# Ten moves in the order of work of a three-layer transformer kernel: rotations, first loads, a bias table, norms and idle products

## The reference

```
x = layer_norm(x)
for l in (0, 1):
    x = layer_norm(alpha * x + hybrid_mixer(x))            # ln 0
    x = layer_norm(alpha * x + memory_attention(x, mem))   # ln 1
    x = layer_norm(alpha * x + conv_ffn(x))                # ln 2
h = rms_norm(x)
q, kv, kr, dil, mq, gates = split(h @ w_in)                # third layer
x = x + rms_norm(merge(gates, mla(q, kv, kr), dilated(dil), mem_attn(mq, mem_2)) @ w_o)
x = x + rms_norm(conv_ffn(rms_norm(x)))
```

## Time and profile before

| what | value |
|---|---|
| runs shown | 1657.93, 1658.93, 1662.61 us; median 1658.93 |
| the profiled execution | 1660.57 us, span 1658.7 us |
| TensorE busy | 1629.4 us, 98% |
| VectorE, ScalarE, GpSimd busy | 1157.1, 868.7, 40.0 us |
| chain that ended last | TensorE 88%, VectorE 9%, issue 2%, ScalarE 1% |
| weights | 525 loads of 512 KB, 4.3 us to landing at the median |
| memory traffic | 305.84 MB, mean 184 GB/s |

### The profile page before, as it was taken

One profiled execution on the slowest core, in us unless ns is written; L12 is line 12 of the kernel. 1 busy time (PEld: TensorE's weight loads), 2 busy tenths in 40 slices (PEclk: granted clock), 3 DMA queues, 4 the chain that ended last, 5 costly groups with the idle time before them and its releaser, 6 DMA issues.

```text
span 1658.7 us, 32250 instructions
## 1 busy us (share of the span) xinstructions
PE 1629.4 (98%) x13674; PEld 1591.4 (96%) x13674; DVE 1157.1 (70%) x1734; ACT 868.7 (52%) x1302; POOL 40.0 (2%) x59
## 2 busy tenths in 40 slices
PE   9999999999999999999999999999999999999998
PEld 8999999999999999999999999998989999999998
DVE  6678778657566767877874966677576545877777
ACT  5456544645444454555355654445745555465554
POOL 3000000003000000000000000000000000000000
PEclk9999999999999999999999999999999999999999
DMA  9854457536656465545664465555545454546562
GB/s 314 288 178 153 153 196 249 187 126 193 227 175 207 161 236 163 162 144 190 203 239 144 160 222 181 201 181 164 178 146 167 152 178 140 179 153 204 178 205 100
DMA packets 82798, 305.84 MB, mean 184 GB/s; under 512 B 10688, under 2 KB 10816, under 8 KB 80480
## 3 DMA queue, kind: packets, MB, share of 16 engines
q1 hardware_dynamic: 77008, 279.44, 50.7%
q0 software_dynamic: 5648, 24.35, 4.9%
HBM read 300.52 MB, written 6.29 MB: 185 GB/s over the span
## 4 chain that ended last, share of the span: by engine, by line
PE 88%; DVE 9%; issue 2%; ACT 1%; DVEq 0%; ACTq 0%
PE general L617 55%; PE general L621 14%; PE scores L659 5%; DVE weights_lo L1584 3%; PE attention_out L659 3%; PE probs_transposed L659 3%; PE attention_out L811 2%; PE scores L744 1%; PE probs_transposed L763 1%; PE scores L835 1%; ACT weights_hi L1154 1%; PE general L690 1%; PE probs_transposed L617 1%; DVE x_tok L1655 1%; DVE x_tok L1652 1%
## 5 line engine op out<-in xcount | busy, mean ns | idle before, releaser
L1584 DVE TENSOR_TENSOR weights_lo<-raw_weights,weights_hi 128x1024 fp32r<-128x1024 f32 x525 | 633.5, 1222 | 387.0 <-ACT weights_hi L1154 384.9
L1154 ACT ACTIVATE weights_hi<-raw_weights 128x1024 fp32r<-128x1024 f32 x525 | 553.3, 1057 | 402.3 <-PE general L617 227.2
L617 PE MATMUL general<-xT_hi_part,weights_hi 128*128 128x256 f32 x2432 | 682.8, 281 | 5.2 <-DVE weights_lo L1584 2.7
L617 PE MATMUL general<-xT_lo_part,weights_hi 128*128 128x256 f32 x2432 | 675.7, 278 | 0.0
L617 PE MATMUL general<-xT_hi_part,weights_lo 128*128 128x256 f32 x2432 | 675.6, 278 | 0.0
L617 PEld LDWEIGHTS general<-xT_hi_part,weights_hi 128*128 128x128 f32 x2432 | 458.8, 189 | 13.6 <-issue 8.5
L617 PEld LDWEIGHTS general<-xT_lo_part,weights_hi 128*128 128x128 f32 x2432 | 458.4, 188 | 0.4
L617 PEld LDWEIGHTS general<-xT_hi_part,weights_lo 128*128 128x128 f32 x2432 | 458.4, 189 | 0.0
L1927 DVE SCALAR_TENSOR_TENSOR exp_ring<-general,param_cols,exp_ring 128x255 f32<-128x255 f32 (+1 forms) x176 | 76.7, 477 | 43.4 <-ACT exp_ring L1343 41.9
L1343 ACT ACTIVATE exp_ring<-general,param_cols 128x256 f32<-128x256 f32 x88 | 44.9, 561 | 66.5 <-PE general L617 66.4
L621 PE MATMUL general<-weights_hi,xT_hi_part 128*128 128x256 f32 x272 | 76.9, 283 | 1.0 <-DVE xT_lo_part L1615 1.0
(11 more groups left out here) (318 smaller groups left out, 2935.3 us busy)
## 6 DMA issues: line engine op xcount, KB each, us to landing
raw_weights<-in_stream SPq DMA_DIRECT2D x525, 512.0 KB, 4.3
attention_area<-in_ln_rows POOLq DMA_DIRECT2D x9, 1024.0 KB, 5.4
bias_scratch<-in_rpb POOLq DMA_DIRECT2D x32, 96.0 KB, 11.8
attention_area<-bias_scratch POOLq DMA_DIRECT2D x2, 1536.0 KB, 8.2
memT_hi<-memT_scratch POOLq DMA_DIRECT2D x2, 1024.0 KB, 5.3
memT_lo<-memT_scratch POOLq DMA_DIRECT2D x2, 1024.0 KB, 9.0
attention_area<-in_mem SPq DMA_DIRECT2D x1, 1024.0 KB, 5.2
z_tok<-in_x SPq DMA_DIRECT2D x1, 1024.0 KB, 8.9
```

Of the source, the lines that this page charges most:

```text
L617: ins = nc.tensor.matmul(ps[b][0:m, half * T:half * T + T], w[wk][:, half * m:half * m + m], x[xk_], start=first, stop=last, skip_group_ch ...
L1154: nc.scalar.activation(hi_half(h), raw_half(h), ACT.Copy).then_inc(*hi_done.more())
L1584: nc.vector.tensor_tensor(lo_half(h), raw_half(h), hi_half(h).bitcast(F32), ALU.subtract).then_inc(*lo_done.more())
```

## The change

- A: the prologue loads half 0, then mem in two pieces (of 512 columns), halves 1 and 2, then x. Both engines split half 0 before the memory's transposes; VectorE makes the low of half 2 before the norm's statistics.
- B: in l0 and l1 the order is rot0, rot1, qn0, rot2, rot3, qn1, and ScalarE's exponential for lambda comes between the two qn.
- C: differential attention multiplies with the values three steps behind.
- D: the first tile of the memory output waits for one head less, and kc 2 waits for the other.
- E: `build_bias(1)` is issued in l0 right after the first table has been read and the memory parts saved.
- F: at the border of l0 and l1, xk 2 is evacuated before two of the splits, and `next_x` splits as far as ("xk", 3) needs between its two tiles.
- G: in the third layer's first norm each tile has its own root, the second tile is squared and scaled by halves, and mv 1 and the first gains come without splits before them.
- H: gate 7 stands between the second and the third rotation of the third layer.
- I: in the third layer the latent attention's output stays in natural order; gates, dilated and memory outputs are put into it as they are read, and the merge's casts work on whole blocks.
- J: `keep_busy(36)` becomes `keep_busy(20)`.

The diff, cut to what the list speaks of:

```diff
-            elif stage.kind == "layer":
+            else:
                 at, parts, src = i // 2, YB, po[:, 0:T]
-            else:
-                return [grouped(part[:, i // 2, :]) for part in YB], spread(po[:, 0:T])
+            if name == "mem":
+                return [natural(part[:, i, :]) for part in parts], regrouped(src)
...
-                    if step >= 2 and name not in ("na", "mla"):
+                    if name == "da":
+                        if step >= 3:
+                            values(js[step - 3])
+                    elif step >= 2 and name not in ("na", "mla"):
...
-            pe.wait_ge(*memin.at(0))
-            to_feature("memT", mem_tok)
+            for i in range(DC // 2):
+                if i % 2 == 0:
+                    pe.wait_ge(*(memin, memrest)[i // 2].at(0))
+                transposes(("memT", i), mem_tok, 2 * i)
...
                                          raw[:, 2 * n:2 * n + 2, :], start=True, stop=True).then_inc(*full[b].more())
-                for i in range(2):
-                    linear(("qn", i), XT, DC, True)
+                    if n % 2:
+                        linear(("qn", n // 2), XT, DC, True)
...
                     if kc == 0:
+                        pe.wait_ge(*po_read.at(NUM["layer"][2][16]))
+                    if kc == 2:
                         pe.wait_ge(*po_read.at(NUM["layer"][2][17]))
-                    if kc == 2:
...
-            for key in (("gate", 7), ("dq", 0), ("dq", 1)):
+                if i == 1:
+                    filler(("gate", 7))
+            for key in (("dq", 0), ("dq", 1)):
...
-            keep_busy(36)
+            keep_busy(20)
...
                 for k in range(DC):
-                    reach((name, k // 2))
+                    if k >= 4:
+                        split_to(AT[(stage.name, (name, k // 2))] + 2 * (k // 2) - 2)
...
-                    nc.scalar.activation(yT3[:, c, :], po[:, 0:T], ACT.Copy).then_inc(*po_read.more())
+                    dst, src = yT3[:, c, :], po[:, 0:T]
+                    if name == "dil":
+                        dst, src = natural(dst), regrouped(src)
...
-                    if step >= 2 and name != "dil":
+                    if name == "da" and step >= 3:
+                        attn_out(js[step - 3])
+                    if step >= 2 and name != "dil" and (name != "da" or step == len(js) + 1):
...
+            split_to(1)
             for i in range(DC // 2):
                 act.wait_ge(*when_full(("memT", i)))
                 src = bank_of(("memT", i))
                 nc.scalar.activation(MT[0][:, 2 * i:2 * i + 2, :], src[:, :].rearrange("p (c w) -> p c w", w=T),
                                      ACT.Copy).then_inc(*mem_hi.more())
-                if i == 0:
-                    split_to(1)
...
                     layer_norm(2)
-                    filler(("xk", 2))
+                    split_to(AT[(stage.name, ("xk", 2))] + SPLIT - 2)
+                    act.wait_ge(*when_full(("xk", 2)))
+                    nc.scalar.activation(xk[:, 4:6, :], bank_of(("xk", 2))[:, :].rearrange("p (c w) -> p c w", w=T),
+                                         ACT.Copy).then_inc(*read(("xk", 2)))
...
-            mean_square(x3, D, 0, (x_tile0, -1), (x_ready, -1))
-            scale_tile1(0, z3[:, 1, :], x3[:, 1, :], nst[:, 17:18])
-            filler(("mv", 1))
+            act.wait_ge(*x_tile0.at(-1))
+            nc.scalar.activation(junk[:, 0, :], x3[:, 0, :], ACT.Square,
+                                 accum_out=nst[:, 0:1]).then_inc(*squares_done.more())
+            act.wait_ge(*squares_done.last())
+            nc.scalar.activation(nst[:, 8:9], nst[:, 0:1], ACT.Sqrt, bias=cconst("eps_rms"),
+                                 scale=1.0 / D).then_inc(*std_ready.more())
+            for c in range(2):
+                part = slice(c * 512, c * 512 + 512)
+                act.wait_ge(*(x_half, x_ready)[c].at(-1))
+                nc.scalar.activation(junk[:, 1, part], x3[:, 1, part], ACT.Square,
+                                     accum_out=nst[:, 1 + c:2 + c]).then_inc(*squares_done.more())
+            act.wait_ge(*squares_done.last())
+            act.wait_ge(*sums_ready.at(0))
+            nc.scalar.activation(nst[:, 9:10], nst[:, 2:3], ACT.Sqrt, bias=nst[:, 3:4],
+                                 scale=1.0 / D).then_inc(*std_ready.more())
+            act.wait_ge(*norm_factors.at(0))
+            nc.scalar.activation(z3[:, 1, 512:D], x3[:, 1, 512:D], ACT.Copy,
+                                 scale=nst[:, 17:18]).then_inc(*xhat1.more())
+            evacuate_only(("mv", 1), mv[:, :, T:2 * T])
...
-            def next_x(n):
+            def next_x(n, within=None):
 
                 dve.wait_ge(*rows_in.at(n))
                 for t in range(2):
+                    if t == 1 and within:
+                        reach(within)
...
+                    at = slice(2 * cb, 2 * cb + 2)
+                    nc.vector.tensor_scalar(MG[0][:, at, :], acc, 0.5, None, ALU.mult).then_inc(*merge_step.more())
...
+            split_to(1)
             for i in range(DC // 2):
...
-                if i == 0:
-                    split_to(1)
-            split_to(2)
+            split_to(3)
...
-                    next_x(2)
+                    next_x(2, ("xk", 3))
...
+            dve.wait_ge(*x_ready.at(-1))
+            dve.wait_ge(*std_ready.at(0))
+            nc.vector.reciprocal(nst[:, 16:17], nst[:, 8:9]).then_inc(*dve_step.more())
+            dve.wait_ge(*dve_step.last())
+            nc.vector.tensor_scalar(z3[:, 0, :], x3[:, 0, :], nst[:, 16:17], None, ALU.mult).then_inc(*xhat0.more())
+            dve.wait_ge(*squares_done.at(1))
+            nc.vector.tensor_scalar(nst[:, 3:4], nst[:, 1:2], 1.0 / D, EPS_RMS, ALU.mult,
+                                    ALU.add).then_inc(*sums_ready.more())
+            dve.wait_ge(*std_ready.at(1))
+            nc.vector.reciprocal(nst[:, 17:18], nst[:, 9:10]).then_inc(*norm_factors.more())
+            dve.wait_ge(*norm_factors.last())
+            nc.vector.tensor_scalar(z3[:, 1, 0:512], x3[:, 1, 0:512], nst[:, 17:18], None,
+                                    ALU.mult).then_inc(*xhat1.more())
...
+                    pool.wait_ge(*bias_in.at(0))
+                    pool.wait_ge(*mt_saved.at(1))
+                    build_bias(1)
...
-                    build_bias(1)
...
-            sp.dma_start(mem_tok, a["mem"].rearrange("b (t p) d -> p (b t) d", p=P)).then_inc(*memin.more())
-            for h in range(2):
+            load_half(0)
+            for c in range(2):
+                part = slice(c * 512, c * 512 + 512)
+                sp.dma_start(mem_tok[:, :, part], a["mem"][:, :, part].rearrange("b (t p) d -> p (b t) d", p=P)
+                             ).then_inc(*(memin, memrest)[c].more())
+            for h in (1, 2):
```

## The result

The changed kernel takes 1635.9 us at the median of four runs (1635.08 to 1637.07), the kernel before in the same comparison 1659.01: a ratio of 0.9862, 95% interval 0.9849 to 0.9874. That is 23.1 us less. The profiled execution has a span of 1634.2 us against 1658.7, 24.5 less.

The account below looks back on a forecast made before the run. The prediction took TensorE, busy 98% of the span, to bound the kernel. Its ten terms summed to 25.25 us, taken off the median of 1658.93 for a forecast of 1634 us, range 1629 to 1643.

Parts of the forecast that it names:

- two signs it named for being wrong: Whole kernel: total TensorE idle time staying over 15 us, or a low clock remaining at two places.
- R1: Layer 0, the gather's new place: it collides with weight loads there; price 2.3 to 3.8 us, chance 0.15.
- R2: After the rotations or before the last transposes: the clock falls all the same; price 1.7 to 3.4 us, chance 0.15.
- R3: Several places: covered waits come back behind the next late thing; 1640 us, or 1644 with VectorE late; chance 0.13.
- R4: Layer 0's differential attention: the weights' ring runs dry beside the gather; slower than before, 1662.8 us, chance 0.01.
- R5: Memory output: the change doesn't do what it says, its new wait being as late; 2.9 us less gain, chance 0.03.

Follow-up runs that it names:

- gather_alone: The kernel before with only layer 1's bias-table gathers issued early, in layer 0 behind the first table's copy; ratio 0.9979 in ten runs.
- idle_0: The changed kernel without any idle products between the output block and the transposes of the FFN's norm; span 1637.2 us against 1634.2.
- rotations_filled: The kernel before with idle products filling TensorE's two waits around the third layer's fifth rotation; span 1654.2 us against 1658.7.
- idle_36: The changed kernel with 36 idle calls again instead of 20; span 1638.0 us against 1634.2.
- all_three: The changed kernel with low parts made inside next_x and memory loaded in one piece; median 1632.35 us in five runs, ratio to the kernel before 0.9841.
- values_two_behind: The changed kernel with differential attention's values two steps behind again; span 1637.1 us against 1634.2.
- low_inside_next_x: The changed kernel with next_x always making a weights' low part between its tiles, a second at the layers' border; span 1629.3 us against 1634.2.
- gate7_behind: The changed kernel with gate 7 put back behind the third layer's five rotations; span 1637.7 us against 1634.2.

## Why the prediction was right

The forecast was 1634 with a range of 1629 to 1643, and 1635.9 was measured. The sum was 25.25; the trace gave 24.5 and the medians 23.1.

Its method was right: with TensorE busy for 98%, each stall taken away came back in full, but for the part of F's that was forecast to return, and nine of ten parts lie within 0.5 us of their terms. H, its largest, was right in both halves, stalls and clock; C, D, E, F, I and J came within 0.2 of their terms in the trace. Of the two signs it named for being wrong, neither came: TensorE's idle time is 14.0 us, not over 15, and no low clock is left before the last three microseconds, when the products are done.

Mis-sized terms, by size:

- **A** was 1.9 and brought 0.6 in this pair of traces, 0.9 over all. The step that failed is that the norm comes forward by one low (1.2) and an estimated 0.7: it came forward by 0.1 (18.73 against 18.84), because x lands 2.7 us later behind half 2. Mem in two pieces is part of it: half 1, with the same bytes ahead of it as before, lands 1.0 us later on the mean, so half 2 was early by only 1.2 us (11.6 against 12.8) and half 3 late by 1.4. The lower bound of 1.0 was too high as well.
- **B** was 1.65 and is worth 1.9 by the rows of the undo (1.7 in the steps, with the pitch in them). The bound from above was too low: a stall costs its bracket and 0.16, and here another 0.11 by which the second product after it comes late.
- **G** was 2.7 and brought 2.7, then lost 0.5 within two halves: a wait of 0.2 at 1133 that was not there before with 0.1 behind it, and a change of pitch. So it is worth 2.2 to 2.4.
- **D** brought 1.35 a layer where the sum had 1.45. The stall went in full (1.62 at halves 104 and 282), and 0.28 of it was lost again behind the twelfth product, where the wait for the second head and the third head's work now stand.
- **F** was 1.8 and brought 1.6. That the low part of the next half, which can't come earlier, would make the next wait was the one prediction of a new wait, and it is there at the half named, with 0.96 in the brackets against the expected 1.1. In the eight other traces with the same code at this place F brings 1.5 to 1.6 too.

Of the rivals, **R1** (the gathers collide) is refuted by `gather_alone`: the loads do slow (to 10.0 us in the changed kernel), and TensorE does not wait. The Trainium skill's page "DMA: Bandwidth & Descriptors", section "Queues, rings and completion order", has each DMA engine take turns between its queues, packet by packet; the landings, slowed in either place, agree. The step from there to lost time is the prediction's own and not the page's, and it depends on how long each load has until its split: 1.2 us at the least in the new place, nothing in the old. **R2** (the clock) did not come true in the changed kernel, which is at full clock through both places, but `idle_0` and `rotations_filled` show that it was near: with 20 calls fewer it costs 2.2 us. Here the trace agrees with the Trainium skill's page "TensorE: Matmul & The Clock Gate", section "HAM oscillation — how this bites in real kernels", for the idle TensorE of 4.56 us; that the clock of a TensorE that never idles falls as well, behind products on 32 rows, is shown here by the rows of `rotations_filled`. **R3** (waits return behind the next late thing) is true of F, as forecast, and of D and G by 0.3 each. **R4** and **R5** did not happen.

What was luck: E's 1.5 us for the low clock is a thing of some executions, as the stall of 1.74 us without it shows, so a sum made from one trace carried a part that another trace of the same code need not have. The difference between 24.5 (trace) and 23.1 (medians) is of that size, 1.4: the profiled execution of the kernel before, at 1660.57, is one with the low clock. The prediction saw that it lay 1.6 above the median and still took the whole term of 3.8 off the median. A's shortfall of 1.0 to 1.3 also had B's small surplus of 0.2 against it.

## What to carry to other kernels

Where one engine is busy all the time, list its stalls from its timeline, and ask of each what other engine's instruction ends it and whether work that needs nothing can stand there; the gain is the stall and a little more (0.16 to 0.27 us here). A record that is drawn long is no cost by itself: count from start to start. A background transfer is best put where the stream beside it has lead to spare, which is read by setting landings beside first uses: the landings slow down either way. Idle products should end where the operand arrives. A row of products on a quarter of the array's rows brought the clock down here as a pause did, so put a full product in its midst.

## What the runs showed of the hardware that I had not expected

**A matmul has two pitches at one clock.** In long rows of the same three matmuls on 128 x 256, at full clock, one starts every 117.7 ns in some stretches and every 113.3 ns in others. The same products (layer 1, half 229) in the kernel before, nine matmuls apart, and in the changed kernel, nine apart:

```profile
729.76 0.28 PE L617 MATMUL general<-xT_hi_part,weights_hi 128*128 128x256 f32 x1
...
730.82 0.28 PE L617 MATMUL general<-xT_hi_part,weights_hi 128*128 128x256 f32 x1
```

```profile
720.01 0.28 PE L621 MATMUL general<-xT_hi_part,weights_hi 128*128 128x256 f32 x1
...
721.03 0.28 PE L621 MATMUL general<-xT_hi_part,weights_hi 128*128 128x256 f32 x1
```

That is 1.06 us against 1.02. Of the 525 halves, 229 are at the fast pitch in all fourteen traces and 119 at the slow one in all; 168 differ from trace to trace, and nine change within the half. Part of it therefore goes with the place in the program. In the conv FFN, where nothing stands between the products, four halves of up products (L621) are fast and the two of down products behind them (L663) slow, over and over; nine matmuls apart in the changed kernel:

```profile
463.89 0.28 PE L621 MATMUL general<-xT_hi_part,weights_hi 128*128 128x256 f32 x1
...
464.91 0.28 PE L621 MATMUL general<-xT_hi_part,weights_hi 128*128 128x256 f32 x1
...
472.06 0.28 PE L663 MATMUL scores<-weights_hi,ffn_act_hi 128*128 128x256 f32 x1
...
473.11 0.28 PE L663 MATMUL scores<-weights_hi,ffn_act_hi 128*128 128x256 f32 x1
```

The rest goes with the execution: halves 118 to 123, the same code, were fast in the changed kernel's trace and slow in `idle_36`. Counting starts that follow the one before by 116 to 120 ns, there are 4943 in the changed kernel and 5050 in the kernel before, but only 4472 in `rotations_filled` and 4502 in `all_three`: at 4.4 ns each, 1.9 us between the changed kernel and `all_three`, 2.5 between the kernel before and `rotations_filled`. It made `values_two_behind` look some 0.6 us worse and `low_inside_next_x` 1.4 us better than their edits. What decides the pitch I did not find. All slow starts of the changed kernel together cost 21.7 us (4943 x 4.4 ns), nearly what all ten moves brought, but no run shows that the halves that are slow in every trace can be had faster.

**The clock can fall without any idle time**, as in `rotations_filled`, behind the row of products on 32 rows. It stayed low for 3.41 us there and at 412 us in the kernel before, and for 6.83 us at the rotations in the kernel before, in `gather_alone` and in `gate7_behind`, and in `idle_0`. A stall of 2.11 us had it fall at 412 us; one of 1.74 us at the same place, in `rotations_filled`, did not.

**The start scatters.** Half 0's first product starts between 8.9 and 10.7 us with the same prologue, 1.7 us apart, with the landing of the first loads. A part that is worth less than 1 us at the start can't be read from one pair of traces.
